# Mixer's context side under the last product-key chunks, and first products of three stages by halves of the tokens

## The reference, cut to what matters

```
for l in range(2):                                    # first block
    h = x @ w_in[l] + b_in[l]                         # 1024 x 2328
    y_lru = rg_lru(...)                               # conv, gates, scan: 512 wide
    y_nsa = nsa(...)                                  # three-branch attention: 512 wide
    mix = concat(rms(y_lru), rms(y_nsa)) @ w_out[l]
    x = layer_norm(ALPHA * x + mix)                   # "mix" norm
    x = layer_norm(ALPHA * x + peer(x))               # "peer" norm
# peer: q = x @ wq (1024 x 2048); scores of q against 2 x 128 sub-keys;
#       top 16 of each side, top 16 of their 256 sums, per token and head;
#       y = sum over the chosen of 16384 experts: gate * gelu(x . u[e]) * v[e]

h_lat = rmsnorm(x)   * (1 + mod_lat[1]) + mod_lat[0]  # second block
h_ctx = rmsnorm(ctx) * (1 + mod_ctx[1]) + mod_ctx[0]  # ctx: an input, 256 tokens
lat, ctx = h_lat @ w_in_2, h_ctx @ w_in_2             # w_q, w_kv, w_hg, w_gm are its columns
x = x + mod_lat[2] * token_mixer(...)                 # latent attention + gated recurrence
x = x + mod_lat[5] * moe_ffn(...)                     # 32 experts, top 4, all loaded
return rmsnorm(x)
```

## Time and profile before

| what | value |
|---|---|
| median of three runs | 3992.12 us (3991.05 to 3992.42) |
| the profiled execution | 3994.03 us, its span 3992.2 us |
| PE, matmuls | 3738.5 us busy (94%) |
| DVE | 1940.2 us (49%) |
| ACT | 1100.2 us (28%) |
| POOL | 315.6 us (8%) |
| mean granted TensorE clock | 0.97 |
| loaded from memory | 846 MB |
| product keys to mixing 1 / mixing 1 to product keys | about 1097 / 1284 us into the span |
| product keys to mixer | about 2197 us into the span |

### The profile page before, as it was taken

One profiled execution on the slowest core, in us unless ns is written; L12 is line 12 of the kernel. 1 busy time (PEld: TensorE's weight loads), 2 busy tenths in 40 slices (PEclk: granted clock), 3 DMA queues, 4 the chain that ended last, 5 costly groups with the idle time before them and its releaser, 6 DMA issues.

```text
span 3992.2 us, 58689 instructions
## 1 busy us (share of the span) xinstructions
PE 3738.5 (94%) x25080; PEld 2649.9 (66%) x25080; DVE 1940.2 (49%) x3526; ACT 1100.2 (28%) x1715; POOL 315.6 (8%) x205
## 2 busy tenths in 40 slices
PE   8999999999989999999999699898799999999998
PEld 6689889898876898898988465656653333333333
DVE  4585666768555856767685324445522111111111
ACT  2323244444523232444445112233210000000001
POOL 0013200000000132000000000111100000000000
PEclk9899999999988999999999899999889999999999
DMA  4535344444435343344444322111259999999996
GB/s 189 222 127 169 128 149 167 160 174 172 172 128 221 128 169 127 145 168 165 171 171 146 123 90 95 50 56 64 110 223 414 427 428 427 428 427 428 428 427 269
DMA packets 80748, 846.44 MB, mean 212 GB/s; under 512 B 8864, under 2 KB 11040, under 8 KB 12224
## 3 DMA queue, kind: packets, MB, share of 16 engines
q1 hardware_dynamic: 80480, 842.60, 53.9%
HBM read 841.52 MB, written 1.05 MB: 211 GB/s over the span
## 4 chain that ended last, share of the span: by engine, by line
PE 78%; DMA 12%; DVE 8%; ACT 2%; issue 1%; POOL 0%; DVEq 0%; ACTq 0%; SPq 0%
PE bank L85 77%; DMA ring<-in_w_gu_dram 11%; DVE arena L121 2%; PE bank L98 1%; ACT arena L111 1%; DVE arena L135 1%; DVE arena L189 1%; DVE arena L183 1%; DVE arena L153 0%; DVE arena L129 0%; DVE arena L195 0%; DVE arena L147 0%; DVE arena L165 0%; ACT L111 0%; DMA ring<-in_w_inA_dram 0%
## 5 line engine op out<-in xcount | busy, mean ns | idle before, releaser
L85 PE MATMUL bank<-arena 128*128 128x32 bf16 (+9 forms) x10060 | 983.0, 298 | 60.7 <-DVE arena L121 43.1
L85 PEld LDWEIGHTS bank<-arena 128*128 128x128 bf16 (+4 forms) x10060 | 558.7, 125 | 478.9 <-issue 343.7
L111 ACT ACTIVATE arena<-bank 128x256 f32<-128x256 f32 (+2 forms) x499 | 229.6, 460 | 1534.8 <-PE bank L85 1325.5
L121 DVE TENSOR_TENSOR arena<-arena 128x512 bf16<-128x512 bf16 (+5 forms) x894 | 557.1, 657 | 99.5 <-ACT arena L111 85.3
L85 PE MATMUL bank<-ring,arena 128*64 128x512 f32 (+1 forms) x1968 | 502.8, 595 | 40.6 <-DMA ring<-in_w_gu_dram 38.9
L85 PE MATMUL bank<-xT,ring 128*128 128x256 f32 x2016 | 463.1, 388 | 13.7 <-DMA ring<-in_w_inA_dram 11.5
L85 PE MATMUL bank<-xhi,uhi 128*128 128x256 f32 x1552 | 453.5, 292 | 14.5 <-DVE arena L127 8.7
L85 PE MATMUL bank<-xlo,uhi 128*128 128x256 f32 x1552 | 437.2, 282 | 0.0
L85 PE MATMUL bank<-xhi,ring_rounded 128*128 128x256 f32 x1552 | 435.0, 280 | 0.0
L85 PEld LDWEIGHTS bank<-xT,ring 128*128 128x128 f32 x2016 | 386.7, 195 | 67.0 <-issue 11.4
L85 PEld LDWEIGHTS bank<-ring,arena 128*64 128x64 f32 (+1 forms) x1968 | 170.4, 144 | 362.3 <-issue 280.3
(11 more groups left out here) (123 smaller groups left out, 2919.4 us busy)
## 6 DMA issues: line engine op xcount, KB each, us to landing
ring<-in_w_gu_dram SPq DMA_DIRECT2D x97, 2048.0 KB, 24.3
ring<-in_peer_u_dram SPq DMA_DIRECT2D x128, 1024.0 KB, 6.9
ring<-in_peer_v_dram SPq DMA_DIRECT2D x128, 1024.0 KB, 5.0
arena<-in_w_dn_dram SPq DMA_DIRECT2D x62, 2048.0 KB, 22.4
arena<-in_w_gu_dram SPq DMA_DIRECT2D x43, 2048.0 KB, 22.3
ring<-in_w_hg_dram SPq DMA_DIRECT2D x14, 2048.0 KB, 7.7
ring<-in_w_mod_dram SPq DMA_DIRECT2D x12, 2048.0 KB, 7.8
ring<-in_w_inA_dram SPq DMA_DIRECT2D x8, 2048.0 KB, 8.2
```

Source lines behind the costliest of these rows:

```text
L85: i = self.e.matmul(o, l, r, start=start, stop=stop)
L111: self.e.activation(o, i, f, scale=scale, **kw).then_inc(self.sem, 1)
L121: self.e.tensor_tensor(o, a, b, op).then_inc(self.sem, 1)
```

## The change

At three places the stage's first products are made for the half of the tokens that is normed first, while the other half's norm goes on.

- Mixing to product keys (both layers): `pe_mixing` ends with transposes of a half and `pe_query(l, tk, 0)`: piece tk of wq for the first half of the tokens, both after ("xT got", 0). `pe_peer` begins with pieces 0 and 1 for the second half, and then runs the loop over j. The transposes here go through `turn_banks` (banks 6 and 7), the products through `route_banks` (0 to 5); `Slots.follow` takes over the tenants that the banks had.
- Product keys to mixing 1: in the same way with pieces 2 and 3 of `w_inA` (`pe_in_half`).
- Product keys 1 to mixer: the context side moves into the chunk loop of layer 1: S loads `qq` and `ctxT` behind chunk 110's loads, once chunk 109's activations are split (`mixer_free` counts the space of the arena that is free by then); A squares at chunk 112, P sums behind chunk 114, A takes the root at chunk 115, V makes `coef` and the reciprocal behind chunk 116, G scales, A shifts two of eight blocks at each of chunks 120 to 123. Under the last norm P multiplies w_kv by the context in three products between transposes and sums of the x side, which is now squared, summed, scaled and shifted by halves. A squares x and adds the shift, V multiplies by reciprocal and `coef` in one operation. w_kv is then multiplied for each half of x as it comes, and the mixer stage starts with w_q. S no longer waits for the last norm with the mixer's first loads, and w_kv comes first.

```diff
+
+    def follow(self, other, first):
+
+        self.n, self.tenant = 0, other.tenant[first:first + len(self.bufs)]
...
+        route_banks = Slots(bank[0:6], at)
+        turn_banks = Slots(bank[6:8], at)
...
+        def pe_in_half(l, j, tk):
+            P.wait_ge(*at["landed", ("w_inA", l, j)])
+            w = ring.of("w_inA", l, j)[:, 0:PIECE].rearrange("p (c n) -> p c n", c=8)
+            ts_ = slice(tk * 128, tk * 128 + 128)
+            for half in range(2):
+                if tk == 0:
+                    b, (s, n) = banks.take("in", l, j, half)
+                    P.wait_ge(s, n)
+                b = banks.of("in", l, j, half)
+                for k in range(2):
+                    ct = half * 2 + k
+                    P.mm(b[:, k * 256 + tk * 128:k * 256 + tk * 128 + 128],
+                         [(w[:, dc, ct * 128:ct * 128 + 128], xT[:, dc, ts_]) for dc in range(8)])
+                if tk:
+                    P.mark("in", l, j, half)
+            if tk:
+                ring.back(P, "w_inA", l, j)
...
-                for half in range(2):
-                    pe_in(l, j, half)
+            if l == 0:
+                banks.restart()
+                P.wait_ge(*at["landed", ("xT",)])
+                for j in (2, 3):
+                    for half in range(2):
+                        pe_in(l, j, half)
+            else:
+                for j in (2, 3):
+                    pe_in_half(l, j, 1)
...
-            layer_norm_pe(x3, "mix", l)
+
+            route_banks.follow(banks, 0)
+            turn_banks.follow(banks, 6)
+            for tk in range(2):
+                to_xT_pe(x3, tk, turn_banks, "mix", l)
+                P.wait_ge(*at["xT got", 0, "mix", l])
+                pe_query(l, tk, 0)
...
+                if l and c == AHEAD:
+                    sp_context()
...
+        def pe_query(l, j, tk=None):
+            P.wait_ge(*at["landed", ("wq", l, j)])
+            w = ring.of("wq", l, j)[:, 0:PIECE].rearrange("p (c n) -> p c n", c=8)
+            t0, t1 = (0, 256) if tk is None else (tk * 128, tk * 128 + 128)
+            for hf in range(2):
+                if tk != 1:
+                    b, (s, n) = route_banks.take("q", l, j, hf)
+                    P.wait_ge(s, n)
+                b = route_banks.of("q", l, j, hf)
+                for k in range(2):
+                    ct = hf * 2 + k
+                    P.mm(b[:, k * 256 + t0:k * 256 + t1],
+                         [(w[:, dc, ct * 128:ct * 128 + 128], xT[:, dc, t0:t1]) for dc in range(8)])
+                if tk != 0:
+                    P.mark("q", l, j, hf)
+            if tk != 0:
+                ring.back(P, "wq", l, j)
+
...
-            route_banks.restart()
+            for j in range(2):
+                pe_query(l, j, 1)
             for j in range(4):
...
+                if j >= 2:
+                    pe_query(l, j)
...
+                if l and c == AHEAD + 4:
+                    pe_context_sum()
             banks.restart()
             banks.n = 4
-            layer_norm_pe(x3, "peer", l)
+            if l:
+                pe_mixer_first()
+            else:
+                for tk in range(2):
+                    to_xT_pe(x3, tk, banks, "peer", l)
+                    P.wait_ge(*at["xT got", 0, "peer", l])
+                    pe_in_half(l + 1, 2 + tk, 0)
...
+                if l and c == AHEAD + 6:
+                    dve_context()
             layer_norm_dve(lambda tk, dh: dve_add_sum(l, tk, dh), pz, ("ln2", l), p_lst, p_mv, x3, "peer", l)
+            if l:
+                dve_mixer_first()
...
+                if l:
+                    act_context(c - AHEAD)
+            if l:
+                act_mixer_first()
+            else:
+                layer_norm_act(p_mv, banks, "peer", l)
...
+            if l:
+                pool_context()
...
+
+        def act_context(i):
+            if i == 2:
+                after_h(A)
+                A.wait_ge(*at["landed", ("ctxT",)])
+                A.act(x_sq[1], cT, ACT.Square)
+                A.mark("squares", "c")
+            if i == 5:
+                A.wait_ge(*at["rms sum", "c"])
+                A.act(x_rstd[:, 256:512], bank[6][:, 0:256], ACT.Sqrt, scale=1.0 / 1024, bias=eps6)
+                A.mark("rms root", "c")
+            if 10 <= i < 14:
+                A.wait_ge(*at["c scaled"])
+                for c in (2 * (i - 10), 2 * (i - 10) + 1):
+                    A.act(hT[:, c, 256:512], x_sq[1][:, c, :], ACT.Identity, bias=mod[:, c, 1:2], scale=coef[:, 1, c:c + 1])
+            if i == 13:
+                A.mark("h ctx")
+
+        def pe_context_sum():
+            P.wait_ge(*at["squares", "c"])
+            P.wait_ge(*at["gelu", 1, 126])
+            P.mm(bank[6][:, 0:256], [(ones, x_sq[1][:, i, :]) for i in range(8)])
+            P.mark("rms sum", "c")
+
+        def dve_context():
+            V.wait_ge(*at["landed", ("qq",)])
+            for k, (g, j, v) in enumerate(((Q_NMG, 8, 0), (Q_NMG, 8, 1), (Q_NFG, 32, 0))):
+                V.stt(coef[:, k, :], mod[:, j:j + 8, v], 1.0, par(g, 8), ADD, MUL)
+            dve_rms(x_rstd[:, 256:512], "c")
+            V.mark("c rstd")
...
+        def pe_kv(ct, t0, n_):
+            P.wait_ge(*at["landed", ("w_kv",)])
+            w = ring.of("w_kv")[:, 0:3072].rearrange("p (c n) -> p c n", c=8)
+            P.mm(banks.of("proj", ct, "w_kv")[:, t0:t0 + n_],
+                 [(w[:, dc, ct * 128:ct * 128 + 128], hT[:, dc, t0:t0 + n_]) for dc in range(8)])
...
+        def pe_mixer_first():
+            x_turns = Slots([bank[i] for i in (4, 0, 2, 3)], at)
+            banks.take("xT", 0, 0, "peer", 1)
+            for ct in (2, 0, 1):
+                banks.take("proj", ct, "w_kv")
+            banks.take("xT", 4, 0, "peer", 1)
+            banks.take("rms", "x")
+            for a in (0, 4):
+                banks.take("xT", a, 1, "peer", 1)
+            P.wait_ge(*at["h ctx"])
+            pe_kv(0, 256, 256)
+            to_xT_pe(x3, 0, x_turns, "peer", 1)
+            pe_kv(1, 256, 256)
+            pe_x_sum(0)
+            to_xT_pe(x3, 1, x_turns, "peer", 1)
+            pe_kv(2, 256, 256)
+            pe_x_sum(1)
+            for tk in range(2):
+                P.wait_ge(*at["h lat", tk])
+                for ct in range(3):
+                    pe_kv(ct, tk * 128, 128)
+                    if tk:
+                        P.mark("proj", ct, "w_kv")
+            ring.back(P, "w_kv")
+
+        def dve_mixer_first():
+            for tk in range(2):
+                ts_ = slice(tk * 128, tk * 128 + 128)
+                V.wait_ge(*at["rms root", "x", tk])
+                V.recip(x_rstd[:, ts_], x_rstd[:, ts_])
+                V.wait_ge(*at["xT got", tk, "peer", 1])
+                for c in range(8):
+                    V.stt(x_sq[0][:, c, ts_], x_rstd[:, ts_], coef[:, 0, c:c + 1], xT[:, c, ts_], MUL, MUL, lag=c)
+                V.mark("x scaled", tk)
...
+        def act_mixer_first():
+            def root(tk):
+                ts_ = slice(tk * 128, tk * 128 + 128)
+                A.wait_ge(*at["rms sum", "x", tk])
+                A.act(x_rstd[:, ts_], banks.of("rms", "x")[:, ts_], ACT.Sqrt, scale=1.0 / 1024, bias=eps6)
+                A.mark("rms root", "x", tk)
+
+            def squares(tk):
+                to_xT_act(tk, banks, "peer", 1)
+                A.act(half_of(x_sq[0], tk), half_of(xT, tk), ACT.Square)
+                A.mark("squares", "x", tk)
+
+            def shifted(tk):
+                ts_ = slice(tk * 128, tk * 128 + 128)
+                A.wait_ge(*at["x scaled", tk])
+                for c in range(8):
+                    A.act(hT[:, c, ts_], x_sq[0][:, c, ts_], ACT.Identity, bias=mod[:, c, 0:1])
+                A.mark("h lat", tk)
+
+            ln_std_act(p_mv, 0, "peer", 1)
+            squares(0)
+            ln_std_act(p_mv, 1, "peer", 1)
+            root(0)
+            squares(1)
+            shifted(0)
+            root(1)
+            shifted(1)
+            banks.back(A, "rms", "x")
...
         def sp_mixer():
-            after_stage(S, "peer", 1)
-            once(pp[:, 0:NQ_COLS], d["qq"], "qq")
-            once(cT, d["ctxT"].rearrange("(c p) t -> p c t", p=128), "ctxT")
+            load(d["w_kv"], 3072, "w_kv")
             for j in range(2):
                 load(d["w_q"][j], 3072, "w_q", j)
-            load(d["w_kv"], 3072, "w_kv")
...
+            after_stage(S, "peer", 1)
...
         def pe_mixer():
-            banks.restart()
             after_stage(P, "peer", 1)
-            P.wait_ge(*at["landed", ("qq",)])
-            pe_rms(x_sq[0], 256, "x")
-            pe_rms(x_sq[1], 256, "c")
-            P.wait_ge(*at["h lat"])
-            P.wait_ge(*at["h ctx"])
             for j in range(2):
                 pe_project(3, 256, 8, hT, "w_q", j)
-            pe_project(3, 512, 8, hT, "w_kv")
...
-            V.tt(x_sq[0], xT, xT, MUL)
-            V.mark("squares", "x")
-            dve_rms(x_rstd[:, 0:256], "x")
```

(17 more changed lines are left out.)

75 lines of the change are left out of this document (36 added, 39 removed).

## The result

The changed kernel takes 3967.9 us (3964.0 to 3970.9, 4 runs) against 3992.3 us (3991.1 to 3992.4, 4 runs): 24.4 us less, ratio 0.9940 with a 95% interval of 0.9929 to 0.9952. So the two profiles differ by 29.9 us, 5.5 more than the medians.

What follows compares the result with a forecast made beforehand. The expert stage is bound by its loads, so PE's path at the seams before it moves the end. 15.0 - 2.0 - 28.4 = -15.4 us from a median of 3992.1 gives 3977 us, range 3958 to 3987.

Steps and rivals of the forecast that it cites:

- Mixing to product keys: Seam in both layers: first key scores 10.3 us later delay DVE's choice of experts, +7.5 us per layer, +15.0 both.
- Product keys to mixing: Seam passed once: half pieces of w_inA during the norm bring pe_tok earlier, -2.0 us (0 to -3.5).
- The bound: Expert stage bound by its loads at 427 GB/s from 2890 us on; PE's path before 2870 moves the end equally.
- the slow restart: PE's slow products after standing 7 us before the transposes of the chosen: between 0 and 2.9 us, taken as 2.4.
- ACT's table: In DVE's choice of experts: ACT has its exponential table in by then, giving back 0.7 us.
- no slow start is left: Seam mixing to product keys: PE's products run without a slow start, since no gap is over 1.1 us.
- Rival 1: Choice of experts not on the path: each layer gains 2.1 us in place of losing 7.5, 3958 us; chance 0.10.
- the half product: Half a piece (32 products of 128 columns) on PE at the seams takes 7.6 us, a whole one 13.8.
- In the loop: Layer 1's product-key loop: the moved context sum costs 3.45 us and POOL's scaling 3.0.
- POOL's lock: Layer 1's loop: POOL's context scaling holds DVE's splits 4.4 us, PE's path +3.0 us (0 to +5.5).
- Seam to the mixer: Last loop product to w_q and w_kv done: 53.2 us in place of 88.0, a gain of 34.8 (30 to 37).
- a gap of one or two us shows no such fall: PE at the seams: slow products of 2.9 us follow some four idle us, but not one or two.

Runs made afterwards that it cites:

- experiment 3: Changed kernel with the first key scores right behind the second half of piece 0, before the second half of piece 1: 3951.0 us, ratio 0.9898 to the kernel before.
- experiment 1: Changed kernel with pieces 0 and 1 of wq whole again between mixing and product keys: 3954.0 us, ratio 0.9908 to the kernel before.
- experiment 2: Kernel before with only pieces 0 and 1 of wq by halves, in both layers: 4003.0 us, ratio 1.0027 to the kernel before.
- experiment 4: Changed kernel with only piece 0 of wq by halves, pieces 1 to 3 whole: 3944.6 us, ratio 0.9886 to the kernel before.
- experiment 5: Changed kernel with the transposes of the chosen keys behind 26 chunks in place of 24: 3950.2 us, ratio 0.9908 to the kernel before.
- Experiment 7: Changed kernel with POOL's scaling of the context in four operations in place of one: 3965.3 us, 24.5 under the kernel before.

## Why the prediction was right, and where it was off

**The bound was right.** PE's path over the seams, read up to the experts, gives the result; the experts' stage took 1124.3 us from the end of its first wait to the end of the span before and 1123.8 after. One reading under it was wrong: the loads don't run at 427 GB/s from 2890 on. In the profile of the kernel before it was 85 GB/s from 2900 to 2925, 313 from 2950 to 2975, and 427 only from 3050 on. The sum doesn't use it.

**Mixing to product keys: mechanism right, size too large.** Step by step: first half piece 1287.3 forecast, 1287.51 measured; first scores 1318.9 and 1319.02; second scores 1323.0 and 1322.91; start of the choice 1321.6 and 1321.63; end of DVE's work 1446.7 and 1445.18; PE's stand 7 and 5.60. The terms that were off: DVE made up 4.1 us (from 127.7 us for the choice to 123.6), not 2.6; its copy of the transposes came 4.0 us late (1446.18 for 1442.19), not 5.1, and the transposes themselves 3.6, not 5.0; and the slow restart cost 1.4 (4.9 us late at the next chunk, less 3.6), not 2.4. Of the 4.1 us, 1.9 are the copy and 0.7 ACT's table, both as forecast. The other 1.5 are a second pair of operations that stood behind a split of POOL before and no longer does (DVE's timelines, before and changed):

```profile
1428.13 1.93 DVE L127 TENSOR_SCALAR arena<-arena 128x32 uint32<-128x32 uint32 x2
```

```profile
1438.52 0.40 DVE L128 TENSOR_SCALAR arena<-arena 128x32 uint32<-128x32 uint32 x2
```

That the first scores came at the forecast time was luck, two errors that cancel. Four half pieces take 29.0 us, not 30.4, and the transposes 0.9, not 1.1; but the step "no slow start is left" failed in this execution: the first half piece took 8.87 us where the same one took 7.25 in experiment 3 and in the second profile of the changed kernel. In that profile the scores come 32.8 us after the last output product, not 34.4. Experiments 1 and 2 put both layers together at 11 us where I had 15. Rival 1 (the choice not on the path, 3958) would have needed PE to go on at the transposes; it doesn't. What it supposed, no stand before the transposes, is what experiments 3 to 5 bring about, and there the gain is there too.

**Product keys to mixing: -3.7 where I had -2.0.** The mis-sized term is the half product: three half pieces in a row took 21.8 us at both seams (192 passes, as from 1297.26 to 1319.02), 7.25 each, not 7.6. I had it from the eight scores' products, 0.236 us each; in a row of 64 passes they take 0.227. No run takes this part back by itself, but the profiles agree: the stretch takes 38.95 and 37.95 us in the two kernels without it, and 34.5 to 35.4 in the nine profiles with both pieces by halves.

**In the loop: +5.2 where I had +6.45.** From the context's sum to the loop's end it takes 41.5 us, of which 13 chunks of 2.79 are 36.3. The sum costs its 3.45 (3.62 in the row). POOL's lock came where it was forecast, and DVE was held 4.5 us, as against 4.4, but PE waited 1.65 us, not 3.0: the buffers had more lead. Experiment 7 shows that 1.2 of it is POOL's whole instruction.

**Seam to the mixer: -36.05 where I had -34.8.** h of the first half was there 17.6 us after the loop (18.2 forecast), of the second 24.7 (25.9), w_q done at 51.9 (53.2). The 1.2 us are shorter small operations: eight of ACT's shifts took 3.44 us, 0.43 each, not 0.52 (ACT's timeline, changed kernel).

```profile
2220.84 3.44 ACT L112 ACTIVATE arena<-arena,mod 128x128 f32<-128x128 f32 x8 [0.77 <-DVE arena L136]
```

**What was not in the sum.** The two profiles of the changed kernel lie 14.5 and 9.0 us below the forecast difference of -15.4. The stretches that the change touches give 8.0 and 6.6 of it, by the terms above. The other 2 to 6 us come from stretches that the change doesn't touch: mixing 1 took 143.7 us before, 140.7 in the changed kernel, and 138.8 to 145.0 in the other eleven profiles, all with the same products in it. The rows show what differs: the same operation at one or the other level of the clock (the granted clock was 0.72 from 2626 to 2632 us before), as here the first products after a stand of 2.22 us, twice in the kernel before, then in the changed one at the first of the two places:

```profile
2627.53 3.68 PE L85 MATMUL bank<-arena 128*128 128x128 f32 x16 [2.22 <-DVE arena L121]
...
2642.09 2.05 PE L85 MATMUL bank<-arena 128*128 128x128 f32 x16 [2.22 <-DVE arena L121]
```

```profile
2600.03 2.05 PE L86 MATMUL bank<-arena 128*128 128x128 f32 x16 [2.22 <-DVE arena L122]
```

Such an event is worth 1.6 us, sometimes in two parts (2.51 and 3.38 us at these two places in the second profile of the changed kernel). So the profile that the prediction was read from already spoke against "a gap of one or two us shows no such fall". Whether the change makes them rarer by itself, or shifts them by chance, is left open: the four runs of the changed kernel stand in two pairs, at 3964 and 3971 us.

## What to carry to other kernels

When a stage is cut so that its first products start earlier, look at what the first result of the old order starts on another engine. Here four half pieces ahead of the first scores filled PE's gap of 4 us and put a choice of 124 us off by 10, with a slack of 3; the same four with the scores put in between, or one half piece, keep the gain. Where PE has no other work, as at the seam to the mixer, work by halves and work that doesn't depend on the norm both pay: 10 and 26 us at the seam, less the 5 that the moved work costs in the loop.

## What was not expected of the hardware

Stands of PE of 2.2 us and less were followed by products at the lower level at one time and not at another, in one and the same program; I had taken it that gaps of one or two us are safe. Two rows of the kernel before show it for 2.22 us (3.68 and 2.05 us for the same 16 passes, above). The changed kernel shows it for two stands in a row, of some 0.85 and 0.94 us: the first half piece of layer 1 took 8.87 us in its first profile (granted clock 0.61 from 1287 to 1290) and 7.25 in its second (1.00 from 1288 to 1291).

```profile
1288.00 7.41 PE L86 MATMUL bank<-xT,ring 128*128 128x128 f32 x64 [0.94 <-ACT xT L112]
```

By the Trainium skill ("TensorE: Matmul & The Clock Gate", Part 1: The HAM clock gate) the number of matmuls at the lower level varies between runs of one kernel. The trace agrees, with the 8.87 and 7.25 us of the changed kernel.

And DVE's choice, an unbroken row of some 120 us, takes 2.9 us more in one execution of a program than in another (layer 1 of the changed kernel: 123.6 and 126.5 us, PE's stand 5.60 and 8.65), though it began 1.6 us earlier after the last output product where it took longer. The rows tell where this lies. Both have the same 477 operations and the same idle time. Compared with the same operation elsewhere, five rows are longer by 8.3 us in the first profile and six by 11.3 in the second, and each of them lies beside one of POOL's dozen splits of 2.4 us. In the kernel before it was seven rows and 11.7 us, and in layer 1 of experiment 1, with the scores as soon after the last output product as there, five and 7.2. So what the choice costs hangs on which of its operations meet a split; no run took the splits away.
